# Halving the hand-overs of norms, head outputs and the last product in a diffusion backbone with expert retrieval

## The chip, the cores and the metric

One core of one Trainium2 chip runs the whole kernel. The metric is device time in microseconds, the median of several executions. The profile is one more execution of the same program. Engines are named as in the profile: PE (TensorE, matmuls), PEld (its weight loads), DVE (VectorE), ACT (ScalarE), POOL (GpSimd), SP (SyncE, which here only issues transfers).

## What is computed

Two layers over 256 context tokens and 256 latent tokens of width 1024, all in float32, in tiles of 128 tokens. The reference, cut to its loop:

```python
for l in range(DEPTH):                       # DEPTH = 2
    sh1, sc1, g1, sh2, sc2, g2 = split(silu(c) @ w_ada[l] + b_ada[l], 6)
    h  = rmsnorm(x,  norm_attn_g[l]) * (1 + sc1)  + sh1
    hc = rmsnorm(xc, norm_attn_g[l]) * (1 + sc1c) + sh1c
    y, yc = parallel_mixers(h, hc, ...)      # in projection, MLA (8 heads) and differential (4 heads)
                                             # attention, subnorm of the latter, output projection
    x = x + g1 * y
    h = rmsnorm(x, norm_ffn_g[l]) * (1 + sc2) + sh2
    x = x + g2 * peer_ffn(h, p)              # per token: 8 heads x 16 of 16384 experts, rows u and v
    if not last:                             # the same for the context tokens
        ...
return rmsnorm(x, final_norm_g)
```

`peer_ffn` takes, for each token and each of its 128 picks, a row u (1024) and a row v (1024) of the layer's expert tables: `sum over picks of gelu(u . h) * gate * v`.

## The kernel before

The residual stream X stays on chip as four tiles of 128 tokens x 1024 (0 and 1 the context, 2 and 3 the latent tokens). There are six expert blocks: both pairs in layer 0, the latent pair in layer 1. A block is 128 slots; one slot gathers one expert row pair (8 KB) for each of the 128 tokens, 1 MB, by an indirect transfer of POOL (L681) into a ring of 8 buffers called EXPERT. DVE forms the dot product (L1595), ACT the gelu, the weight and, for three slots of four, a diagonal matrix (L1169, L1171, L1176), PE multiplies that with the v half (L985), and DVE adds the fourth slot itself (L1605). The buffer is then free for the transfer eight slots later.

Everything else is background: norms, projections, attention, the picks of experts. Each engine runs its instructions in one order, written by a planner. `make_plan` lists stages; `front`, `attention` and `outward` give a tile's stages, `weave` mixes slots into them by costs (COST), `keeps_gates` holds a block's close out of the stages between the gates and the use of their rows, and `late` moves slots forward in the orders of DVE and ACT. Three stretches have no slots to mix in: the start until the first picks are there, the pause between the layers (block 3 closed, block 4 without picks), and the end.

The stages that matter here, with their lines:

- `stat` and `norm`. ACT squares X over 1024 columns with a row sum (L1051), takes the root (L1052), DVE inverts it (L1285), ACT scales X into XN (L1063), PE transposes XN in two groups of four 128x128 tiles (L773), and ACT writes them to HT with scale and shift, eight instructions of 128x128 (L1074). PE waits for the whole of XN, and the products that read HT (L844 for the projections, L975 for the expert query) wait for all eight. In `product` that wait is written as a wait for the last bank PE filled, so that it also covers ACT's copies after a `turn` (L1099), which the next product doesn't read.
- `gates`, `hnorm`, `heads`, `out`. DVE puts the gate g1 on diagonals (GD, L1221, called by `diagonals`), PE spreads it to rows by eight matmul records of ones x GD (L860), DVE copies the rows to GROW (L1487). This is done ahead of each half of the output projection (`out` part 0), 512 columns at a time. `hnorm` normalizes the differential heads (L1461, L1126), `heads` transposes the head outputs O, and ACT copies them to HT in two halves (L1135, L1137). After a half of the projection DVE multiplies by GROW and adds to X; only the second half signals `x_ready`.
- `close` adds a block's result to X in two halves, and signals after the second.
- `pick` and `more` are the expert query (two groups of eight products of 128x128), the scores, and the choice of the 16 best.
- `last` is the final norm of a latent tile: square, root, one product over 1024 columns on DVE (L1657), one store of 512 KB (L655).
- `ada`, `adae`, `adat`, `mod` form the modulation vectors from w_ada, 1 MB pieces staged in the EXPERT ring; `adae` is ACT's copy of a product (L1047).

ACT holds one table of functions; where the next function isn't in it, the profile shows ACT_TABLE_LOAD at the line of the instruction that needs it.

## Time and profile before

| | |
|---|---|
| median of 3 runs | 2654.83 us (2645.4 to 2659.23) |
| profiled execution | 2648.58 us, of which span 2645.9 us |
| PE, DVE, ACT, POOL busy | 2068.0, 1854.0, 1149.7, 975.7 us |
| moved by DMA | 980.26 MB, mean 370 GB/s |
| start without slots | 0 to about 238 us |
| pause between the layers | about 1771 to 1915 us |
| last slot's weights to the end | about 2632 to 2646 us |

The busy shares (78% of the span for PE, 70% for DVE) are means over stretches with different limits, and none of them says by itself what sets the time. The page's 40 slices show the DMA engines nine tenths busy or more nearly everywhere but in the three stretches of the table. The chain that ended last puts 21% on transfers, 32% on PE, 25% on DVE and 12% on ACT.

### The profile page before, as it was taken

To read this page: it belongs to the slowest core of one execution; us is meant where nothing else is said; L and a number is where in the kernel's file an instruction comes from. 1 tells how busy PE (TensorE), PEld (TensorE's weight loads), DVE (VectorE), ACT (ScalarE), POOL (GpSimd) and SP (SyncE) were. 2 spreads that over 40 slices of the span, in tenths; PEclk is the share of its full clock that TensorE was granted. 3 is DMA by queue.
4 is the path that set the end of the run, shared out by engine and by line. 5 is a ranking of instruction groups with operands and counts; after the bars stand their busy time and mean duration, and the time that the engine had idled before them with its cause. 6 is when DMAs were issued, how large, how long until landed. Compare 5 with 4: busy or idle time off the path is not lost.

```text
span 2645.9 us, 26377 instructions
## 1 busy us (share of the span) xinstructions
PE 2068.0 (78%) x6888; PEld 1083.2 (41%) x6888; DVE 1854.0 (70%) x4486; ACT 1149.7 (43%) x3047; POOL 975.7 (37%) x916
## 2 busy tenths in 40 slices
PE   5997787876978877888777697879777887677766
PEld 2455443543444445444334244334543444333322
DVE  0146986895557878885979765654597786867776
ACT  2123494344236644753433723432245654433332
POOL 1012333332434333543343444420133443445553
PEclk8998888888989988989889998989888988888988
DMA  8587999997999999999999999996599999999997
GB/s 338 159 298 293 387 385 387 396 395 299 382 389 391 363 409 390 382 383 411 412 409 390 402 415 405 398 405 234 184 412 388 415 351 394 415 382 420 422 421 308
DMA packets 215418, 980.26 MB, mean 370 GB/s; under 512 B 17628, under 2 KB 75512, under 8 KB 116984
## 3 DMA queue, kind: packets, MB, share of 16 engines
q0 software_dynamic: 123648, 855.69, 79.6%
q1 hardware_dynamic: 91640, 123.05, 13.6%
q8 instruction: 55, 0.90, 0.1%
q14 instruction: 75, 0.61, 0.1%
HBM read 977.62 MB, written 1.05 MB: 370 GB/s over the span
## 4 chain that ended last, share of the span: by engine, by line
PE 32%; DVE 25%; DMA 21%; ACT 12%; issue 8%; POOL 1%; SPq 0%; POOLq 0%; DVEq 0%; ACTq 0%
DMA EXPERT<-in_peer_uv,FIX 20%; PE VS L985 12%; PE PA L844 9%; DVE EXPERT L1595 8%; DVE ACC L1605 3%; DVE SCR L1221 2%; PE PA L872 2%; PE PB L773 1%; PE PB L975 1%; ACT L1169 1%; ACT WEI L1171 1%; PE VS L802 1%; PE PB L912 1%; POOL EXPERT L681 1%; ACT DIAG L1176 1%
## 5 line engine op out<-in xcount | busy, mean ns | idle before, releaser
L985 PE MATMUL VS<-EXPERT,DIAG 128*128 128x512 f32 x2304 | 1174.9, 651 | 253.9 <-ACT DIAG L1176 251.7
L681 POOL DMA_INDIRECT EXPERT<-in_peer_uv,FIX x768 | 901.2, 1173 | 1083.5 <-PE VS L985 704.4
L1595 DVE CUSTOM_DVE_ANT_0 EXPERT<-EXPERT,H 128x1024 f32<-128x1024 f32 x768 | 925.0, 1224 | 327.7 <-DMA EXPERT<-in_peer_uv,FIX 318.2
L985 PEld LDWEIGHTS VS<-EXPERT,DIAG 128*128 128x128 f32 x2304 | 458.0, 210 | 829.0 <-issue 480.0
L1169 ACT ACTIVATE GEL<-DOT 128x1 f32<-128x1 f32 x768 | 155.0, 202 | 1028.1 <-DVE DOT L1595 1013.8
L844 PE MATMUL PA<-WT,HT 128*128 128x512 f32 (+2 forms) x720 | 298.6, 560 | 20.3 <-ACT KTD L1099 7.4
L1605 DVE SCALAR_TENSOR_TENSOR ACC<-EXPERT,WEI,ACC 128x1024 f32<-128x1024 f32 x192 | 245.9, 1281 | 25.9 <-ACT WEI L1171 24.0
L1176 ACT ACTIVATE DIAG<-IDN,WEI 128x128 f32<-128x128 f32 x576 | 231.3, 402 | 62.9 <-PE VS L985 44.5
L975 PE MATMUL PB<-HT,WT 128*128 128x128 f32 (+1 forms) x1472 | 212.7, 305 | 39.9 <-issue 36.3
L1171 ACT ACTIVATE WEI<-GEL,GATE 128x1 f32<-128x1 f32 x768 | 226.3, 295 | 24.9
L975 PEld LDWEIGHTS PB<-HT,WT 128*128 128x128 f32 x1472 | 205.4, 216 | 64.8 <-issue 58.7
L844 PEld LDWEIGHTS PA<-WT,HT 128*128 128x128 f32 x720 | 137.2, 194 | 166.0 <-issue 123.4
L673 POOL COPY FIX<-IDX 128x8 uint32 (+1 forms) x96 | 39.7, 413 | 324.6 <-PE VS L985 224.9
L1169 ACT ACT_TABLE_LOAD x115 | 147.5, 1283 | 6.3 <-ACT SCR L1117 0.4
L773 PE MATMUL PB<-IDN,SCR 128*128 128x128 f32 (+1 forms) x382 | 63.8, 319 | 108.0 <-DVE SCR L1376 26.2
L711 POOL DMA_DIRECT2D EXPERT<-in_w_ada x48 | 34.6, 723 | 233.6 <-PE VS L802 159.8
L773 PEld LDWEIGHTS PB<-IDN,SCR 128*128 128x128 f32 (+1 forms) x382 | 51.3, 160 | 141.0 <-ACT SCR L1063 34.8
L956 PE MATMUL PA<-SKT,SCR 128*128 128x128 f32 x192 | 38.9, 337 | 73.4 <-ACT SCR L1154 73.4
L1117 ACT ACTIVATE SCR<-PB,NM 128x512 f32<-128x512 f32 (+1 forms) x96 | 58.7, 614 | 45.1 <-DVE NM L1440 43.2
L956 PEld LDWEIGHTS PA<-SKT,SCR 128*128 128x128 f32 x192 | 31.7, 229 | 102.6 <-ACT SCR L1154 95.6
L1423 DVE TENSOR_REDUCE MX<-PB 128x1 f32<-128x512 f32 (+1 forms) x96 | 55.5, 597 | 21.2 <-PE PB L912 20.6
L1117 ACT ACT_TABLE_LOAD x50 | 64.2, 1283 | 6.4 <-PE PB L912 5.6
(146 smaller groups left out, 1730.0 us busy)
## 6 DMA issues: line engine op xcount, KB each, us to landing
EXPERT<-in_w_ada POOLq DMA_DIRECT2D x48, 1024.0 KB, 11.3
WT<-in_peer_wq SPq DMA_DIRECT2D x92, 512.0 KB
WT<-in_w_in SPq DMA_DIRECT2D x48, 512.0 KB
WT<-in_w_out SPq DMA_DIRECT2D x48, 512.0 KB
EXPERT<-in_peer_uv,FIX POOLq DMA_INDIRECT x768
WT<-in_w_in SPq DMA_DIRECT2D x16, 384.0 KB
WT<-in_w_in SPq DMA_DIRECT2D x16, 288.0 KB
WT<-in_mla_wq_up SPq DMA_DIRECT2D x4, 512.0 KB
```

The costliest lines, as they stand in the source:

```text
L681: pool.indirect_dma_start(out=EXPERT[:, j, :], out_offset=None, in_=a["peer_uv"], in_offset=bass.IndirectOffsetOnAxis(ap=FIX[:, par, j:j + ...
L773: last = nc.tensor.transpose(bank[0:rows, i * P:(i + 1) * P], s, IDN[:, :])
L844: last = nc.tensor.matmul(bank[:, 0:n], ht(k, t), w[:, k % KP, 0:n], start=(k == 0), stop=(k == KD - 1))
L956: last = nc.tensor.matmul(bank[:, c * P:(c + 1) * P], QP[:, r, c, t * P:(t + 1) * P], SKT[:, 2 * l + c, :], start=True, stop=True)
L975: last = nc.tensor.matmul(bank[:, mine], held["w"][k // HP][:, k % HP, c * P:(c + 1) * P], HT[:, k, mine], start=(k == 0), stop=(k == KD - 1))
L985: ins = nc.tensor.matmul(VSUM[n][:, :], DIAG[:, i, :], EXPERT[:, j, D + n * W:D + (n + 1) * W], start=first, stop=last_one)
L1117: ins = nc.scalar.activation(PR[:, h % 2, c, 0:keys], bank[:, 0:keys], ACT.Exp, bias=NM[:, h % 2, c:c + 1], scale=SC_M if h < MH else SC_D ...
L1169: nc.scalar.activation(GEL[:, one], DOT[:, j:j + 1], ACT.Gelu).then_inc(gelu_ready, 1)
L1171: nc.scalar.activation(WEI[:, one], GEL[:, one], ACT.Copy, scale=gate).then_inc(wei_ready, 1)
L1176: nc.scalar.activation(DIAG[:, i, :], IDN[:, :], ACT.Copy, scale=WEI[:, one]).then_inc(diag_ready, 1)
L1595: nc.vector.tensor_tensor_reduce(out=EXPERT[:, j, 0:D], in0=EXPERT[:, j, 0:D], in1=H2[:, b % HB, :], scale=1.0, scalar=0.0, op0=ALU.mult, ...
L1605: nc.vector.scalar_tensor_tensor(out=ACC[:, :], in0=EXPERT[:, j, D:2 * D], scalar=WEI[:, BY_PE:BY_PE + 1], in1=ACC[:, :], op0=ALU.mult, op ...
```

## The change

1. **Norms by halves.** ACT squares 512 columns at a time. The first sum is scaled and gets the epsilon in an added one-column instruction (into NE), and the root takes the second sum with NE as its bias. XN is written and signalled by halves, PE transposes each as it comes, and `x_ready` counts halves, in `out` and in `close`.
2. **HT by halves.** `half_there` waits for four of the eight pieces of a tile's HT (for the first half of the head outputs likewise), before parts 0 and 2 of a product or before k = 0 and 4 of a first expert query. The wait for the last filled bank is gone from `product`, not from `up`.
3. **Gate rows ahead.** Two stages `rows`, one after `hnorm` and one after `heads`, form both halves of the rows and copy them to a GROW of two halves; `out` no longer does. In the two attentions without slots the `gates` stage moves into the attention (`gates_early`). The planner counts a cost of 10 for each `rows`.
4. **Tables asked for ahead.** `table_of` runs a one-column instruction of the function that comes next, with no input to wait for: the root before the norm after the pause's close and before the last one, the exponential before the first attention of either slot-free stretch.
5. **The final product and its store** in two halves each.

The diff, cut:

```diff
 def attention(l, g, t):
     out = [("attn", l, g, t, i) for i in range(-1, MH + DH + 2)]
-    return out + [("gates", l, g, t), ("hnorm", l, g, t), ("heads", l, g, t)]
+    return out + [("gates", l, g, t), ("hnorm", l, g, t), ("rows", l, g, t, 0), ("heads", l, g, t), ("rows", l, g, t, 1)]
+
+
+def gates_early(stages, after):
+    gates = next(s for s in stages if s[0] == "gates")
+    rest = [s for s in stages if s != gates]
+    return rest[:after] + [gates] + rest[after:]
...
-    return s[0] in ("gates", "hnorm", "heads") or (s[0] == "out" and s[3] == 0)
+    return s[0] in ("gates", "hnorm", "heads") or (s[0] == "rows" and s[4] == 0)
...
-    attend, leave, first = attention(0, CTX, 0), outward(0, CTX, (0,)), pick_apart(0, CTX)[0]
-    plan += mingle(attend[:-2], modulation(0, (3, 4, 5))) + [("mod", 0, 2)]
-    plan += attend[-2:-1] + products(1, 0) + [("adae", 1, 0)] + attend[-1:] + [("adat", 1, 0)]
+    attend, leave, first = gates_early(attention(0, CTX, 0), 4), outward(0, CTX, (0,)), pick_apart(0, CTX)[0]
+    plan += mingle(attend[:-4], modulation(0, (3, 4, 5))) + [("mod", 0, 2)]
+    plan += attend[-4:-2] + products(1, 0) + [("adae", 1, 0)] + attend[-2:] + [("adat", 1, 0)]
...
-    keys, attend, leave = front(1, LAT, (1,), queries=False), attention(1, LAT, 0), outward(1, LAT, (0,))
+    keys, attend, leave = front(1, LAT, (1,), queries=False), gates_early(attention(1, LAT, 0), MH + 3), outward(1, LAT, (0,))
...
-    plan += [("adat", 1, 3), sc2[1]] + attend[MH + 4:-1] + sc2[2:] + [("adae", 1, 4), attend[-1], ("adat", 1, 4), ("mod", 1, 2)]
+    plan += [("adat", 1, 3), sc2[1]] + attend[MH + 4:-2] + sc2[2:] + [("adae", 1, 4)] + attend[-2:] + [("adat", 1, 4), ("mod", 1, 2)]
...
                 if stage[0] == "last":
                     t = stage[1]
-                    sp.wait_ge(y_ready, t + 1)
-                    sp.dma_start(out[0, t * P:(t + 1) * P, :], X[:, 2 + t, :]).then_inc(stored, 16)
+                    for half in range(2):
+                        at = slice(half * W, (half + 1) * W)
+                        sp.wait_ge(y_ready, 2 * t + half + 1)
+                        sp.dma_start(out[0, t * P:(t + 1) * P, at], X[:, 2 + t, at]).then_inc(stored, 16)
...
             def norm(stage):
-                pe.wait_ge(xn_ready, tick("norm"))
                 for half in range(2):
+                    pe.wait_ge(xn_ready, tick("norm"))
                     bank = fill_b()
...
+            def half_there(ts, half):
+                for t in ts:
+                    pe.wait_ge(emptied_b, held["ht", t, half])
...
                 if part == 0:
-                    if kind == "out":
-                        gate_rows()
-                    pe.wait_ge(emptied_b, rb.n)
                     held["banks"] = [fill_a() for t in ts]
                     held["fills"] = ra.n
+                if part % (PARTS // 2) == 0:
+                    half_there(ts, part // (PARTS // 2))
...
                 for k in range(KD):
+                    if first and k % (KD // 2) == 0:
+                        half_there(ts, k // (KD // 2))
...
-            def mean_square(tile, place):
-                link(nc.scalar.activation(place, X[:, tile, :], ACT.Square, accum_out=NS[:, :]))
-                nc.scalar.activation(NQ[:, :], NS[:, :], ACT.Sqrt, scale=1.0 / D, bias=EPST[:, :]).then_inc(root_ready, 1)
+            def mean_square(tile, place, changes):
+                for half in range(2):
+                    at = slice(half * W, (half + 1) * W)
+                    if changes:
+                        act.wait_ge(x_ready[tile], 2 * changes - 1 + half)
+                    link(nc.scalar.activation(place[:, at], X[:, tile, at], ACT.Square, accum_out=NS[:, half:half + 1]))
+                    if half == 0:
+                        nc.scalar.activation(NE[:, :], NS[:, 0:1], ACT.Identity, scale=1.0 / D, bias=EPST[:, :])
+                nc.scalar.activation(NQ[:, :], NS[:, 1:2], ACT.Sqrt, scale=1.0 / D, bias=NE[:, :]).then_inc(root_ready, 1)
...
+                if (l, tile, which) == (1, 3, 1):
+                    table_of(ACT.Sqrt)
...
-                nc.scalar.activation(XN[:, t % 2, :], X[:, tile, :], ACT.Copy, scale=NR[:, :]).then_inc(xn_ready, 1)
+                for half in range(2):
+                    at = slice(half * W, (half + 1) * W)
+                    nc.scalar.activation(XN[:, t % 2, at], X[:, tile, at], ACT.Copy, scale=NR[:, :]).then_inc(xn_ready, 1)
...
+            def table_of(function):
+                nc.scalar.activation(IDLE[:, :], EPST[:, :], function)
...
+                if h == 0 and t == 0 and l == g:
+                    table_of(ACT.Exp)
...
-                act.wait_ge(x_ready[2 + t], 4)
+                if t == 1:
+                    table_of(ACT.Sqrt)
                 tick("norm")
-                mean_square(2 + t, XN[:, t, :])
+                mean_square(2 + t, XN[:, t, :], 4)
...
+            def rows(stage):
+                _, l, g, t, n = stage
+                bank = from_a()
+                if n == 0:
+                    diagonals(l, g, 1, 1)
+                nc.vector.tensor_copy(GROW[:, n, :], bank[:, :]).then_inc(emptied_a, 1)
+                dve.wait_ge(emptied_a, ra.n)
...
-                    tt(YT[:, t, :], bank[:, :], GROW, ALU.mult).then_inc(emptied_a, 1)
+                    tt(YT[:, n, :], bank[:, :], GROW[:, n, :], ALU.mult).then_inc(emptied_a, 1)
                     dve.wait_ge(emptied_a, ra.n)
-                    ins = tt(x, x, YT[:, t, :], ALU.add)
-                    if n == 1:
-                        ins.then_inc(x_ready[2 * g + t], 1)
+                    tt(x, x, YT[:, n, :], ALU.add).then_inc(x_ready[2 * g + t], 1)
...
-                x = X[:, 2 + t, :]
-                nc.vector.scalar_tensor_tensor(out=x, in0=x, scalar=NR[:, :], in1=X[:, 0, :], op0=ALU.mult,
-                                               op1=ALU.mult).then_inc(y_ready, 1)
+                for half in HALVES:
+                    x = X[:, 2 + t, half]
+                    nc.vector.scalar_tensor_tensor(out=x, in0=x, scalar=NR[:, :], in1=X[:, 0, half], op0=ALU.mult,
+                                                   op1=ALU.mult).then_inc(y_ready, 1)
```

## Rows read from the trace of the kernel before

**Rows 1.** Busy time by stretch, in 50 us windows: us, each engine, PEclk, DMA share, GB/s.

```profile
250.00:300.00 50.00, 37.19 (x149) 24.41 (x150) 47.82 (x157) 23.01 (x63) 15.82 (x16) 0.81 1.02 411
...
650.00:700.00 50.00, 40.75 (x97) 18.51 (x98) 34.41 (x54) 15.33 (x52) 18.09 (x16) 0.91 0.82 325
...
1850.00:1900.00 50.00, 42.03 (x255) 27.41 (x254) 19.81 (x63) 13.28 (x29) 0.00 (x0) 0.97 0.41 134
...
2550.00:2600.00 50.00, 34.13 (x62) 12.21 (x61) 30.59 (x45) 15.56 (x54) 30.10 (x22) 0.90 1.01 421
```

**Rows 2.** Chain that ended last: start us, us, what; the first 50 us.

```profile
21.04 1.15 ACT SCR L1051 x2
...
41.59 5.35 ACT HT L1074 x15
```

**Rows 3.** Timeline (start us, us, engine line op, operands, [idle before]): copies ahead of products.

```profile
77.38 1.07 ACT L1099 COPY QTD<-PB 128x512 f32<-128x512 f32 x2 [30.45 <-PE PB L773]
...
78.50 14.00 PE L844 MATMUL PA<-WT,HT 128*128 128x512 f32 x32 [0.73 <-ACT QTD L1099]
...
1803.48 4.15 PE L844 MATMUL PA<-WT,HT 128*128 128x288 f32 x16 [0.68 <-ACT KTD L1099]
```

**Rows 4.** Timeline of 204 to 216 us: second norm of the first tile, first expert query.

```profile
203.98 1.06 ACT L1051 ACTIVATE SCR<-X 128x1024 f32<-128x1024 f32 x1 [17.20 <-DVE X L1221]
...
205.69 1.15 ACT L1063 ACTIVATE SCR<-X,NR 128x1024 f32<-128x1024 f32 x1 [0.23 <-DVE NR L1285]
...
207.64 2.90 ACT L1074 ACTIVATE HT<-PB,MOD 128x128 f32<-128x128 f32 x8 [0.33 <-PE PB L773]
...
210.60 5.47 PE L975 MATMUL PB<-HT,WT 128*128 128x128 f32 x32 [1.83 <-ACT HT L1074]
```

**Rows 5.** Groups of instructions with shapes kept apart: busy us, mean ns | idle before.

```profile
L1154 ACT COPY SCR<-PB 128x128 f32<-128x128 f32 x88 | 22.1, 251 | 60.1 <-PE PB L975 60.0
...
L1047 ACT COPY EXPERT<-VS 128x512 f32<-128x512 f32 x12 | 6.9, 578 | 16.1 <-PE VS L802 15.8
...
L1487 DVE COPY SCR<-PA 128x512 f32<-128x512 f32 x12 | 8.2, 684 | 0.0
```

**Rows 6.** Timeline of 1780 to 1795 us, where the stream has paused between the layers.

```profile
1780.66 1.28 ACT L1052 ACT_TABLE_LOAD   x1
...
1781.96 0.29 ACT L1052 ACTIVATE NQ<-NS,EPST 128x1 f32<-128x1 f32 x1
...
1784.51 2.91 ACT L1074 ACTIVATE HT<-PB,MOD 128x128 f32<-128x128 f32 x8 [0.33 <-PE PB L773]
...
1784.78 1.92 PE L802 MATMUL VS<-EXPERT 128*32 128x512 f32 x16
...
1787.47 7.13 PE L844 MATMUL PA<-WT,HT 128*128 128x512 f32 x16 [0.77 <-ACT HT L1074]
```

**Rows 7.** Timeline of 1819 to 1894 us: attention, projection and first expert query.

```profile
1820.47 0.15 DVE L1440 TENSOR_SCALAR NM<-MX 128x1 f32<-128x1 f32 x1
...
1821.08 0.69 ACT L1117 ACTIVATE SCR<-PB,NM 128x512 f32<-128x512 f32 x1
...
1858.91 0.68 DVE L1221 TENSOR_TENSOR GD<-IDN,MOD 128x512 f32<-128x512 f32 x1
...
1862.23 1.09 PE L773 MATMUL PB<-IDN,SCR 128*128 128x128 f32 x8 [1.72 <-DVE SCR L1221]
...
1873.47 1.05 PE L860 MATMUL PA<-GD,ONES 128*128 128x128 f32 x8
...
1889.57 3.84 PE L975 MATMUL PB<-HT,WT 128*128 128x128 f32 x32 [1.83 <-ACT HT L1074]
```

**Rows 8.** Timeline of the last 8 us.

```profile
2639.65 1.28 ACT L1052 ACT_TABLE_LOAD   x1
...
2641.55 1.28 DVE L1657 SCALAR_TENSOR_TENSOR X<-X,NR 128x1024 f32<-128x1024 f32 x1
...
2642.86 0.36 SPq L655 DMA_DIRECT2D out_y<-X  x1
```

56 lines of the change are left out of this document (25 added, 31 removed).

## The prediction

> **What bounds the kernel now.** I read the busy windows first. While slots run, the DMA engines are the limit: in 44 windows of 50 us from 250 to 1750 and from 1900 to 2600 us (the first, the lowest and the last are in [rows 1]) the DMA share is mostly 0.92 to 1.02, and 1.02 is the most any of them shows. In the lowest, 650 to 700 us, it is 0.82. Against 1.02 the 44 windows miss 84.5 us of full transfer (the sum of (1.02 - share) x 50). In the pause between the layers it is another kernel: the share is 0.41 and PE is busy 42.03 of 50 us. So a microsecond taken from a dependent chain in one of the three stretches without slots should move everything behind it, since the stream then starts earlier and has the same bytes to move; a microsecond taken inside the stream counts only in the 84.5 us. Second I read the chain and the timeline of the three stretches, instruction by instruction, for what ended each wait.
>
> **The change part by part.** The sum is made against the profiled execution, 2648.58 us (span 2645.9), which is 6.25 us below the median of 2654.83 that I predict against; I carry the difference over.
>
> *Price of a half on ACT.* A copy of 128 columns takes 0.251 and one of 512 takes 0.578 us [rows 5], so 512 columns fewer save (0.578 - 0.251) / 384 x 512 = 0.44 us. From 1.06 and 1.15 us [rows 4] a half square is about 0.62 and a half XN 0.71. The square's row sum is read out for 0.10 us more on the chain (1.15 for the pair in [rows 2]). A norm then costs ACT 2 x 0.72 instead of 1.15 for squares, 0.30 for the added one-column instruction (as NQ, 0.29 [rows 6]) and 1.42 instead of 1.15 for XN: 0.86 us more. This is the price; what is gained depends on the place.
>
> *Start, to 47 us.* Both first norms lie on the chain in full, from the landing of ctx [rows 2]: 2 x 0.86 = 1.72 us lost. HT of two tiles is 16 pieces of 0.36 us; the product at the end of [rows 2] waits for all and needs, by halves, only twelve: 4 x 0.36 = 1.43 gained. Net 0.29 lost. Then PE waits twice for ACT's copy after a turn, which the next product doesn't read: 0.73 us [rows 3], and the same 0.73 ahead of the product at 94 us: 1.46 gained. The exponential's table before this attention I cost at nothing: PE runs through there with modulation products. The moved gate rows too: PE has no gap in which to put them, the eight records are only at another place.
>
> *Second norm at 204 us.* The first half square hides under the second half of the projection: 1.15 - 0.72 = 0.43 gained. XN by halves brings nothing: HT follows XN's start by 1.95 us [rows 4] with adae's copy in the shadow of PE's transposes; by halves ACT itself is the limit with 1.42 + 0.58 = 2.00 us: 0.05 lost. The query then begins after four pieces of HT instead of eight, and its first 8 records, 8 x 5.47 / 32 = 1.37 us, lie beside the other four [rows 4]. Together 1.75. The start stretch gives -0.29 + 1.46 + 1.75 = 2.9 us.
>
> *Pause between the layers.* Close and norm: the table load of 1.28 us [rows 6] goes under ACT's wait (ACT is idle for microseconds while DVE closes the block), with the same 0.43 and -0.05: HT starts 1.66 earlier. The product started 2.96 after HT's start [rows 6]; now ACT's fourth piece is there after 1.5, but PE still has transposes until about 0.1 after HT's start and then 1.92 us of modulation products [rows 6], so 2.02: 0.94 gained. Sum 2.6. The wait after the turn of kd: 0.68 [rows 3]. The exponential: its operand NM is there at 1820.62 and it runs at 1821.08 behind its table [rows 7]: 0.43 after an issue gap. The GD product of 0.68 us at 1858.91 leaves hnorm's chain [rows 7] (0.60 there) and goes into the attention, where DVE has little slack: I take 0.5 of it, bounds 0 and 0.6. The rows between both halves of the projection, 0.89 of the 1.05 in [rows 7], go; the first rows fall into PE's wait of 1.72 us ahead of `heads` [rows 7]: 0.89 gained. Norm and query as before, at PE's faster level: 0.43 - 0.05 + 8 x 3.84 / 32 = 1.34 [rows 7]. The pause gives 2.6 + 0.68 + 0.43 + 0.5 + 0.89 + 1.34 = 6.4 us.
>
> *End.* The last table load, 1.28 us [rows 8], goes under the wait; the half square gives 0.43. The product of 1.28 becomes two of about 0.70, so the last store is issued 1.28 + 0.43 - 0.12 = 1.6 us earlier and carries 256 KB less, 0.62 us at the 421 GB/s of the last stream window [rows 1]. Store and semaphore took 2645.9 - 2642.86 = 3.04 us [rows 8]. Two issues of 0.36 us don't collide at 0.7 us distance. 2.2 us.
>
> The table load is 1.28 us in the trace and the root follows it at once (1780.66 + 1.28 = 1781.94, root at 1781.96 [rows 6]). The Trainium skill, "ScalarE: Activation LUTs", section "What ACT_TABLE_LOAD costs", adds a drain of 1.38 us to each switch; by that the pause and the end would each give 1.38 more. The trace shows no such gap; so the sum stays without it.
>
> [...]
>
> *Inside the stream.* Twelve of the 18 norms run there: 12 x 0.86 = 10.3 us more of ACT, whose diagonals PE waits for. On the other side are earlier starts of products (four HT pieces, 1.43 us, per norm that PE waits for), the dropped waits behind `turn`, and a wait fewer between the halves of `out`. Each is cheap where DMA is at 1.02 and counts fully only around the windows like 650 to 700 us. I take 0, bounds 10 lost (all of ACT's extra time on the chain) and 10 gained (a good tenth of the 84.5 us). The two `rows` stages shift slots among stages by a place here and there; also in these bounds.
>
> **Sum:** 2.9 + 6.4 + 2.2 = 11.5 us. 2648.58 - 11.5 = 2637.1 for an execution like the profiled one; **2654.83 - 11.5 = 2643.3 us** for the median.
>
> **The rivals.**
> *The stream gains too.* For it: in the window at 650 us DMA starved behind a product and a close, and the chain there goes through HT and PE. Against: ACT pays 0.86 per norm first. With 10 us of the 84.5: 2643.3 - 10 = 2633.
> *The stream pays.* ACT's 10.3 us land on the chain, because slots queue behind `stat` on ACT: 2643.3 + 10.3 = 2653.6, and the whole change looks like nothing. For it: the places where DMA starves are just those where norms run.
> *Slower: DVE is held at the rows.* DVE now waits for PE's rows between hnorm and heads and again after heads, with PE behind slots in its own order and dots queued behind DVE. Place: the four attentions inside the stream, eight waits. Before, DVE was never idle ahead of the copy to GROW (0.0 [rows 5]), so it came there late. To turn the change into a loss over 0.5% the eight waits have to cost 11.5 + 13.3 = 24.8 us, 3.1 us each, more than a slot's share of the stream; at 4 us each the time would be 2643.3 + 32 = 2675.
> *It doesn't do what it says:* the stretches shorten, but landing pieces of w_ada or weights set the pace in the pause. Against: the share of 0.41 there. It would keep the start and the end, 5.1 us: 2649.7.
>
> **How the numbers follow.** Sum as worked out 0.47; the stream gains 0.23; the stream pays 0.15; weights set the pace 0.09; rows hold DVE 0.06. A difference within 0.5%, 13.3 us, is about what a measurement of this kernel can tell from none; the limit is 2641.6, and the forecast lies 1.7 us inside it. Faster: the gaining rival (0.23) and four tenths of the main case (0.18): 0.41. Slower: 0.05. Same: 0.54. The three runs before spread over 14 us, 7 to each side. Range: from 2643.3 down by 10 for the stream and 3 for a PE that stays at its faster level through the query at 210 us (5.47 against 3.84) and the projection, 2630; up to the paying stream and the runs' own spread, 2656.
>
> **What the profile would show.** A root without a table load at the pause's close and at the end; HT's start 1.7 us sooner after the close; no rows between the halves of `out`; the first gather after the start 2.9 us sooner, the first one after the pause a further 6.4 sooner if the stream is as long as before, last dot to end 2.2 us shorter. What remains of the difference is the stream's: if the two stream stretches are longer, the paying rival was right, if DVE idles ahead of the copies to GROW, the slower one. Wrong would be the forecast if ACT's extra 0.86 us per norm came out differently or if the stream didn't pass an earlier start on.

## The result and the profile after

The changed kernel takes **2630.87 us** (median of 7 runs, 2620.14 to 2639.25), the kernel before beside it 2647.33 (7 runs, 2640.21 to 2659.23). The ratio is 0.9933 with an interval of 0.9905 to 0.9961: faster by 0.67%, 17.7 us (10.3 to 25.1). The forecast was 11.5 us and mostly "within 0.5%"; the time lies in the range, 0.9 us above its lower end. Two more comparisons of the same two kernels on other chips gave 0.9939 and 0.9934. The first interval alone would still hold the 11.5 us; the three weighted together give about 17 us (14 to 20, an estimate from the three intervals), which doesn't.

The forecast time was 2643.3, 12.4 us over the measured one. Some 7.5 of that have nothing to do with the change: the kernel before had a median of 2654.83 in three runs and of 2647.33 in seven.

The profiled execution took 2637.23 us, span 2635.3. In the windows of [rows 1], with the same columns:

```profile
250.00:300.00 50.00, 36.74 (x173) 24.50 (x174) 48.53 (x166) 25.02 (x65) 16.62 (x17) 0.90 1.00 390
650.00:700.00 50.00, 50.00 (x130) 23.03 (x129) 28.53 (x46) 13.14 (x46) 20.35 (x20) 1.00 1.02 410
1850.00:1900.00 50.00, 41.23 (x225) 27.68 (x225) 26.00 (x99) 13.16 (x35) 8.52 (x10) 0.93 0.69 245
2550.00:2600.00 50.00, 31.48 (x60) 11.17 (x59) 30.00 (x46) 15.97 (x55) 30.02 (x23) 0.93 1.01 421
```

The picture is the same; the starved place at 650 us has moved (the lowest window of the first stretch is now 600 to 650 us, share 0.66), and 1850 to 1900 already holds the first gathers of block 4. More can be read from the 768 gathers of POOL, which are the same in every kernel here. Their starts cut a trace into five parts: up to the first gather; the first stretch of stream (first to last gather of blocks 0 to 3); from there to the first gather of block 4 (the pause, with some 15 us of tail before the close); the second stretch; and the rest. Three profiles of each kernel (for before, the one shown, one repeated and `pe_busy` below, whose edit puts 0.7 us in ahead of the first query; for after, the one shown and two repeated):

| us | start | first stretch | pause | second stretch | rest |
|---|---|---|---|---|---|
| before | 226.3, 228.9, 228.1 | 1534.3, 1531.9, 1533.7 | 143.6, 147.9, 145.9 | 712.5, 711.2, 707.3 | 29.2, 29.5, 29.5 |
| after | 216.3, 217.5, 219.5 | 1532.2, 1529.0, 1528.0 | 137.1, 137.2, 137.5 | 722.1, 718.4, 718.3 | 27.6, 27.1, 27.4 |
| mean difference | -9.9 | -3.6 | -8.5 | +9.3 | -2.0 |

So the start gives 9.9 us where 2.9 were forecast, the rest what was forecast (2.2), the pause a little more than forecast (6.4; counted from block 3's close to the first gather of block 4 it went from 129.6, 132.0 and 131.3 to 123.5, 121.9 and 123.4, 8.0 less). The two stretches, forecast at zero, are -3.6 and +9.3: not zero, but of opposite signs. The -3.6 is no more than three profiles of one kernel differ by among themselves, the +9.3 is.

Part of the 9.9 is chance. The first product of PE, which waits for the landing of ctx and for the first norms, starts anywhere from 44.2 to 47.0 us in the profiles below, whatever the kernel. From it to the first gather it is 179.3, 184.1 and 182.2 us before and 171.7, 172.2 and 173.5 after: 9.4 us less by the means, 5.8 by the closest pair.

Start (timeline: start us, us, engine line op, operands, [idle before]). The second norm, against [rows 4]:

```profile
197.21 0.63 ACT L1077 ACTIVATE SCR<-X 128x512 f32<-128x512 f32 x1 [5.82 <-DVE X L1260]
...
198.49 1.33 ACT L1094 ACTIVATE SCR<-X,NR 128x512 f32<-128x512 f32 x2 [0.23 <-DVE NR L1324]
199.73 0.56 ACT L1068 COPY EXPERT<-VS 128x512 f32<-128x512 f32 x1
200.19 2.90 ACT L1110 ACTIVATE HT<-PB,MOD 128x128 f32<-128x128 f32 x8
...
201.84 1.13 PE L996 MATMUL PB<-HT,WT 128*128 128x128 f32 x8 [0.44 <-ACT HT L1110]
203.14 2.94 PE L996 MATMUL PB<-HT,WT 128*128 128x128 f32 x24 [0.17 <-ACT HT L1110]
```

The reader is to see the query begin 1.65 us after HT's start instead of 2.96, and its 24 remaining products take 2.94 us, 0.12 each, where 32 took 5.47, 0.17 each: not only earlier, but at the higher of PE's two clock levels. The granted clock is 1.00 from 197 to 212 us, where before it was 0.83 from 210 to 220.

Pause. The first lines answer to [rows 6], the later ones to [rows 7]:

```profile
1767.61 0.29 ACT L1080 ACTIVATE NQ<-NS,NE 128x1 f32<-128x1 f32 x1
...
1769.91 2.90 ACT L1110 ACTIVATE HT<-PB,MOD 128x128 f32<-128x128 f32 x8
...
1772.76 1.06 PE L814 MATMUL VS<-EXPERT 128*32 128x512 f32 x8 [1.40 <-DMA EXPERT<-in_w_ada]
...
1773.75 1.12 PE L861 MATMUL PA<-WT,HT 128*128 128x512 f32 x2
...
1850.44 13.98 PE L861 MATMUL PA<-WT,HT 128*128 128x512 f32 x32
...
1870.54 1.13 PE L996 MATMUL PB<-HT,WT 128*128 128x128 f32 x8 [0.44 <-ACT HT L1110]
1871.85 2.94 PE L996 MATMUL PB<-HT,WT 128*128 128x128 f32 x24 [0.17 <-ACT HT L1110]
```

No table load lies ahead of the root, and HT starts 7.86 us after the close's first add, against 9.91: 2.05 gained, a little over the forecast 1.66. But the product (L861) follows HT's start by 3.84 us: PE waited 1.40 us for a landing piece of `w_ada` and had then 1.06 us of its product to do. It starts 11.70 us after the close's first add in this profile, and 11.69 to 11.72 in every variant of the changed kernel below but `start_late` (13.20), however HT was handed on. Before it was 12.87 in the profile shown, and 14.05 and 14.02 in the other two. The two halves of the output projection are one group of 32 (13.98 us), with no gate rows between.

End, against [rows 8]:

```profile
2630.56 0.29 ACT L1080 ACTIVATE NQ<-NS,NE 128x1 f32<-128x1 f32 x1
...
2631.16 1.42 DVE L1696 SCALAR_TENSOR_TENSOR X<-X,NR 128x512 f32<-128x512 f32 x2
2631.94 1.02 SPq L667 DMA_DIRECT2D out_y<-X  x2
```

### The profile page after: what moved, and what is told of

Same layout as the page of the kernel before. It is cut to its first block, busy times and chain, and to the rows that moved or that the text cites. A ratio compares the mean times of both kernels' runs of the same rounds, so it can differ in the third digit from the quotient of the medians.

```text
span 2635.3 us, 26515 instructions
## 1 busy us (share of the span) xinstructions
PE 2059.6 (78%) x6888; PEld 1073.0 (41%) x6888; DVE 1854.5 (70%) x4488; ACT 1161.4 (44%) x3122; POOL 976.0 (37%) x916
## 3 DMA queue, kind: packets, MB, share of 16 engines
HBM read 977.62 MB, written 1.05 MB: 371 GB/s over the span
## 4 chain that ended last, share of the span: by engine, by line
PE 29%; DVE 24%; DMA 23%; ACT 15%; issue 9%; POOL 1%; SPq 0%; POOLq 0%; DVEq 0%; ACTq 0%
DMA EXPERT<-in_peer_uv,FIX 20%; PE VS L1006 11%; PE PA L861 9%; DVE EXPERT L1634 7%; DVE ACC L1644 3%; ACT L1207 2%; DVE SCR L1260 2%; PE PA L889 2%; ACT L1155 2%; PE PB L996 2%; ACT WEI L1209 2%; ACT SCR L1155 1%; ACT DIAG L1214 1%; PE PB L785 1%; PE VS L814 1%
## 5 line engine op out<-in xcount | busy, mean ns | idle before, releaser
L861 PE MATMUL PA<-WT,HT 128*128 128x512 f32 (+2 forms) x720 | 297.1, 559 | 12.4 <-DMA WT<-in_w_out 4.0
L1209 ACT ACTIVATE WEI<-GEL,GATE 128x1 f32<-128x1 f32 x768 | 226.3, 295 | 24.9
L861 PEld LDWEIGHTS PA<-WT,HT 128*128 128x128 f32 x720 | 137.0, 193 | 159.0 <-issue 132.7
L1634 DVE DVE_READ_ACCUMULATOR2_ANT DOT<- 128x1 f32 x768 | 63.0, 82 | 0.0
```

Of the source, the lines that this page charges most:

```text
L861: last = nc.tensor.matmul(bank[:, 0:n], ht(k, t), w[:, k % KP, 0:n], start=(k == 0), stop=(k == KD - 1))
L1209: nc.scalar.activation(WEI[:, one], GEL[:, one], ACT.Copy, scale=gate).then_inc(wei_ready, 1)
L1634: nc.vector.tensor_tensor_reduce(out=EXPERT[:, j, 0:D], in0=EXPERT[:, j, 0:D], in1=H2[:, b % HB, :], scale=1.0, scalar=0.0, op0=ALU.mult, ...
```

## The experiments

All are timed against the kernel before on their own chip; ratios carry that comparison, profiles are single executions. Three profiles of one kernel scatter by 2 to 5 us in a stretch (the pause after by 0.4), so a smaller distance in a stretch of a single profile shows nothing. The expectations count differently from the table: the first stretch up to block 3's close (14 us more), the pause from there, and the second stretch up to the last add (some 21 us more).

**Both kernels again.**

> The kernel before once more, for its spread and a second profile. Theory A (the 10.0 us that the start stretch lost between the two profiles, from the span's start to the first gather, are mostly PE's clock level and the landing of ctx, which differ from execution to execution): the first gather is issued anywhere from 218 to 228 us, several us away from 226.3, and the ratio is 1.000 within 0.3%. Theory B (the start is the same in every execution, and the change itself brought all 10 us): the first gather is within 1 us of 226.3.

> The changed kernel once more. Theory A (clock and landing by chance): the first gather is issued somewhere from 216 to 224 us, and the difference to the repeat of the kernel before is 3 to 6 us in the start stretch. Theory B (the change brings all of it): within 1 us of 216.3, 10 us ahead of the kernel before. Both: pause between the layers (from the last dot of block 3 to the first gather of block 4) 6 to 7 us shorter than before, end 2 us shorter, ratio 0.993 within 0.003.

> The changed kernel again, unedited, for the other three to be held against: first gather at 216 to 218, pause 122 to 124, end 5.4, first stretch 1544 to 1546 and second 739 to 744 if the two earlier profiles are typical, 2628 to 2632. If single executions scatter by more than that, the second stretch falls outside, as the 733 of the kernel without tables did.

Measured: 1.0007 (0.9992 to 1.0022) for before, 0.9939 (0.992 to 0.9958) and 0.9934 (0.9915 to 0.9952) for after. Their profiles are in the table above. The start is at least 6.8 us shorter in every pairing of them, so the forecast's 2.9 was wrong and not the profile odd.

**The three parts of the change that hand on by halves or leave a wait out, each undone.**

> The changed kernel with the square over 1024 columns again and no NE instruction; XN, HT and all else stay by halves. By the prediction's price (two half squares and NE cost ACT 0.59 us more than one whole square): start 1.2 us shorter than in the changed kernel, second norms, the pause's close and the end each 0.43 us longer, that is 1.3 us longer together with four such places less the start, so 0.5 us longer in the slot-free stretches. Theory that the stream pays for ACT's time: twelve norms x 0.59 = 7 us shorter in the stream, ratio to the changed kernel 0.9975. Theory that the stream doesn't pay: equal within 0.1%.

```diff
-                for half in range(2):
-                    at = slice(half * W, (half + 1) * W)
...
-                    link(nc.scalar.activation(place[:, at], X[:, tile, at], ACT.Square, accum_out=NS[:, half:half + 1]))
...
+                    act.wait_ge(x_ready[tile], 2 * changes)
+                link(nc.scalar.activation(place, X[:, tile, :], ACT.Square, accum_out=NS[:, 0:1]))
```

Measured: 0.9952 (0.9934 to 0.997), beside 0.9939 for the changed kernel on the same chip: no difference that the intervals can tell. Its first stretch is 1523.5 us, shorter than any of five profiles that have the changed kernel's first stretch (1527.1 to 1532.2), its pause 140.1, 3 us longer. That would fit squares in halves that pay outside the stream and cost inside it, with a sum near nothing, but it isn't shown: `rows_late` below, with its squares in halves, has a first stretch of 1525.2.

> The changed kernel with every wait on HT for all eight pieces; the rest stays. By the prediction: start 1.4 us longer ahead of the first product, 1.4 us longer at the first query, pause 0.9 + 0.9 us longer: 4.6 us in sum. Theory that the earlier start of the query also keeps PE at its 2.4 GHz level there: the query at 200 us runs at 5.5 us for 32 records instead of 3.7, 1.7 us more, 6.3 us in sum. Theory that the stream gains from early HT: another 5 us or more on top.

```diff
-                    pe.wait_ge(emptied_b, held["ht", t, half])
+                    pe.wait_ge(emptied_b, held["ht", t, 1])
```

Measured: 0.9968 (0.9954 to 0.9983), 0.3% or 7.7 us slower than the changed kernel beside it (1 to 14 by the two intervals). The start is 221.9 (2.4 to 5.6 back; 174.9 from the first product, 1.4 to 3.2 back), the pause 141.8 (4.5 back), the second stretch 711.1, as before. By this profile HT by halves is worth its forecast 4.7 us and somewhat more outside the stream, and loses part of it inside.

> The changed kernel with the old wait back: a product whose last bank was filled by a turn, not by the norm, waits until ACT has copied that bank. Theory (forecast): 0.73 us each at two places of the start and 0.68 in the pause come back, first gather at 217.8, pause 124; the stream hides its own: 2 us slower than the changed kernel, 2632. Rival (the start is 10 us shorter, not 3, because PE without these gaps is granted 2.4 GHz through it): first gather at 220 or later with PE granted 0.8 instead of 1.0 around 50 to 110 us, 4 us or more slower.

```diff
                 if part == 0:
+                    if rb.n != held["ht", ts[-1], 1]:
+                        pe.wait_ge(emptied_b, rb.n)
                     held["banks"] = [fill_a() for t in ts]
```

Measured: **0.9984 (0.9967 to 1.0002)**. With this one wait put back nearly the whole gain is gone: the ratio lies 0.5% or 13 us (6 to 20 by the intervals) over the changed kernel's. The theory's 2 us falls. The time is the rival's, but not its reason: PE's granted clock is 1.00 from 50 to 110 us here too. Of its twelve executions nine took 2643 to 2651 us and three 2632 to 2634, as fast as the changed kernel; why is open.

**That wait alone.** The kernel before, with nothing changed but the wait:

> The kernel before with one part of the change alone: a product waits for ACT's copies of its own operand HT, not for the last bank that ACT had to empty (which a turn may have filled). Theory (from the changed kernel with that wait put back, which lost 3 to 4 us in the start and 5 in the first stretch): first gather at 222 to 225 us, first stretch 1542 to 1546, pause 0.7 us shorter, 2636 to 2640. Rival (the wait costs only together with the halves, and the kernel that had it back was slow by where its executions fell): first gather at 226 to 228, first stretch 1548, 2644 to 2646.

```diff
-                    pe.wait_ge(emptied_b, rb.n)
+                    for t in ts:
+                        pe.wait_ge(emptied_b, held["ht", t])
...
+                held["ht", stage[3]] = rb.n
```

(the last line is in `heads`, so that the output projection too waits for its own operand).

Measured: **0.9951 (0.9933 to 0.997)**, 13 us (7.9 to 17.7) from a wait that the forecast had at 1.46 + 0.68 us. The first gather is at 222.1, 5.7 us before the mean of before, 4.2 before the profile shown and 6.8 before the repeated one. Outside the stream the two gaps of 0.73 us explain only a part of that. Two views of each kernel, first of the kernel before (repeated), then of `turn_free`: its products, and PE in a 10 us window (us, PE busy, PEclk, DMA share, GB/s).

```profile
76.87 14.00 PE L844 MATMUL PA<-WT,HT 128*128 128x512 f32 x32 [0.73 <-ACT QTD L1099]
92.47 8.01 PE L844 MATMUL PA<-WT,HT 128*128 128x384 f32 x24 [0.73 <-ACT KTD L1099]
113.74 0.70 PE L773 MATMUL PB<-IDN,SCR 128*128 128x128 f32 x4 [2.26 <-DVE SCR L1376]
114.37 4.48 PE L802 MATMUL VS<-EXPERT 128*32 128x512 f32 x24
```

```profile
110.00:120.00 10.00, 7.74 (x41) 0.83 0.37 126
```

```profile
112.87 0.70 PE L773 MATMUL PB<-IDN,SCR 128*128 128x128 f32 x4 [2.26 <-DVE SCR L1378]
113.50 2.78 PE L802 MATMUL VS<-EXPERT 128*32 128x512 f32 x24
```

```profile
110.00:120.00 10.00, 7.74 (x43) 1.00 0.42 147
```

The same 24 products take 4.48 us behind two idle gaps of 0.73 and one of 2.26, and 2.78 us where only the gap of 2.26 is left: 1.7 us of clock (0.83 and 1.00 granted from 110 to 120). All four profiles with the wait in the start (before three times, `turn_wait`) have 4.28 to 4.48. But of the fourteen without it only nine have 2.78; the other five, two of the changed kernel among them, have 3.87 to 4.11. So behind the gaps the products ran slower each time, and without them part of that still comes in some executions.

The rest of the 6.8 us isn't the wait's. From the small products to a score product in the attention it is 16.58 us in the repeated profile and 13.60 in `turn_free` (148.38 to 161.98), which is clock again; but the profile of before that is shown has both gaps and also 13.60:

```profile
152.58 1.06 PE L812 MATMUL PA<-EXPERT 128*128 128x4 f32 x8 [0.41 <-ACT EXPERT L1047]
...
166.18 0.70 PE L912 MATMUL PB<-KTD,QTD 64*128 64x256 f32 x2 [0.56 <-ACT SCR L1117]
```

Counted from the first product, `turn_free` needs 175.4 us to the first gather, 3.9 less than the fastest profile of before, and `turn_wait` 175.4, 1.9 to 3.7 more than the changed kernel's three. So the wait is worth 2 to 4 us in the start.

Inside the stream the same wait is plain to see. PE idles 9.7 us there behind a turn's copy, ahead of products that don't read it (3.21, 0.28, 5.77 and 0.45 us at 691, 718, 1607 and 2045 us; 10.3 in `turn_wait`, nothing in `turn_free` or after), since ACT's copy stands behind the work of slots (three of them at the longest place). That place, in before, and the same eight products in `turn_free`; then PE in 10 us windows of both:

```profile
1605.29 1.54 ACT L1099 COPY KTD<-PB 128x512 f32<-128x512 f32 x3
...
1606.88 4.21 PE L844 MATMUL PA<-WT,HT 128*128 128x288 f32 x8 [5.77 <-ACT KTD L1099]
```

```profile
1596.24 2.10 PE L845 MATMUL PA<-WT,HT 128*128 128x288 f32 x8
```

```profile
1600.00:1610.00 10.00, 4.23 (x10) 0.72 1.02 421
1610.00:1620.00 10.00, 10.00 (x31) 0.93 0.91 341
```

```profile
1600.00:1610.00 10.00, 8.73 (x26) 1.00 1.02 418
1610.00:1620.00 10.00, 6.88 (x22) 1.00 1.02 415
```

The gap is 5.77 us, the eight products behind it take twice as long, and then the transfers fall behind. Against a share of 1.02 the stretch from 1590 to 1650 us misses 1.2 to 1.9 us of transfer in all five profiles that have the wait there, and at most 0.4 in the thirteen others.

> The changed kernel with the dropped wait behind a turn back in the stream alone, not in the start and the pause. Theory (most of the 12 us that this wait was worth lie in the stretches with slots): first gather and pause as in the changed kernel, time 6 us or more over it, 2636 or more, first stretch 1548 or more. Rival (it is the start, where the wait brought 4 to 6 us, and chance for the rest): within 3 us of the changed kernel.

```diff
+                    quiet = (kind, l, g) == ("in", 0, CTX) or (kind, l, g, ts) in (("out", 0, CTX, (0,)), ("out", 1, LAT, (0,)))
+                    quiet = quiet or ((l, g, ts) == (1, LAT, (1,)) and name in ("kd", "vd", "kv"))
+                    if rb.n != held["ht", ts[-1], 1] and not quiet:
+                        pe.wait_ge(emptied_b, rb.n)
```

Measured: 0.9956 (0.9941 to 0.9971) beside 0.9934: 5.8 us slower, 5.0 by the medians, but the intervals leave anything from 0 to 12. Start (217.7) and pause (137.6) are those of the changed kernel, the first stretch 1535.1 us as in `turn_wait` (1535.2) and 3 over the longest of the changed kernel's (though `mixed_late` below reaches 1535.0 without the wait); the second 721.8 (`turn_wait` 722.8) against 718.3 to 722.1. So some 6 us of the wait's 13 lie in the stream by this estimate, where I had counted its drop as hidden. Of them 1.2 to 1.9 are traced, to the place at 1607 us. Start and pause are longer in `turn_wait` by 2 to 4 and 1 to 3 us.

**Is an earlier start passed on?** The second stretch is 9 us longer after, just about what the pause had become shorter. If the stretch took that back, forecasting by stretches would be wrong at its root.

> The changed kernel with the same 84 more products ahead of the first query of the start instead, 10 us. Theory (passed on in full): first gather at 227, first stretch 1544 to 1546, 10 us over the changed kernel, 2640. Rival (the first stretch absorbs part, because it starves less when its tables of work are further ahead): first stretch under 1540, time under 2636.

> The changed kernel with the eight small products of the last modulation vector in the pause, right ahead of the first query there, done 22 times over (84 more at 0.13 us, 10.8 us of PE on the path to the first gather, 0.4 of it in an idle gap); the results are unchanged. Theory (what comes before a stretch is passed on in full): the pause is 10 us longer, the second stretch as long as in the changed kernel, time 10 us over it, 2640. Rival (the second stretch absorbs it, as it seems to have taken back what the change gained in the pause: before 731 us behind a pause of 131, after 741 behind one of 123): second stretch 732 or less, time 2630 to 2634.

```diff
-                for k in range(4):
+                for k in [0, 1, 2, 3] * (22 if (l, n) == (1, 1) else 1):
```

(and with (1, 5) for `pause_late`).

Measured: 1.0087 (1.0071 to 1.0103) and 1.0075 (1.0059 to 1.0092), 2669.17 and 2667.44 us beside 2631.75. The delay came out three times as large as I had worked out, since the line runs for two operands (168 more products, not 84) and each took 0.20 us:

```profile
201.68 35.23 PE L825 MATMUL PA<-EXPERT 128*128 128x4 f32 x176
236.77 6.27 PE L997 MATMUL PB<-HT,WT 128*128 128x128 f32 x32
```

The question is answered all the same. The first gather of `start_late` is 35.5 us later than the mean of after, its stretches are 1527.1 and 718.3 long, and its time is 37.4 us longer. The pause of `pause_late` is 171.1 against 137.3, 33.8 us longer; its second stretch is 716.0, 2.3 under the shortest of after, and its time 35.7 us longer. Neither stretch absorbs more than the scatter. The rival falls, and "what comes before the stream counts in full" stands.

**The longer second stretch.** If not given back, it is made by the change. Seven profiles whose stream hands HT on by halves (after three times, `turn_wait`, `turn_stream`, `start_late`, `pause_late`) have 716.0 to 722.8; the three of before and `turn_free` 707.3 to 712.5; `ht_whole` 711.1. So HT by halves looked like the part that costs there, 7 us, and in after its distance opened between gathers 104 and 120 of block 4, at a norm (57.2 to 57.5 us against 51.7 to 52.6 before; but `pause_late` and `start_late` are as long in all with 51.7 and 47.3 there).

> The changed kernel, but what follows the last norm inside the second stretch (the one of the second latent tile ahead of its joint queries) waits for the whole HT. Theory (the second stretch is 8 us longer in all kernels with halves of HT in it, and the distance opens between its gathers 104 and 120, where this norm lies): second stretch 732 to 736. Rival (it is the sum of several places, the product of the input projection and that of the output too): second stretch 738 to 744. Start, pause and first stretch as in the changed kernel by both.

```diff
+                if stage[1:] == (1, LAT, 1, 2):
+                    held["ht", stage[3], 0] = rb.n
```

Measured: 0.994 (0.9922 to 0.9959), the second stretch 715.6 by gathers (736.7 from first gather to the last add): between both expectations, and gathers 96 to 112 took 57.2 us as in the changed kernel (57.9), not 52.2 as in `ht_whole`. So that norm isn't shown to be the cause; 715.6 is less than 3 us under the shortest of after.

> The changed kernel, with the halves kept only where no slots run: in the twelve norms and four head outputs inside the two stream stretches the square and XN are one instruction each again and the products wait for the whole HT; the first two squares are whole too. Theory (the halves pay in the stream: extra ACT time in stretch 1, the products that start on half of HT in stretch 2): first gather at 216 to 217 us and pause of 122 to 124 us as in the changed kernel, first stretch 1538 to 1542 as with whole squares, second stretch 732 to 735 as with whole HT waits, so 9 to 16 us faster than the changed kernel: 2614 to 2621. Rival (the second stretch is longer by a shift in where slots and stages meet, whatever its norms do, and stretch 1 differs by chance): second stretch 738 to 744, first 1544 to 1546, time within 3 us of 2630.

```diff
+IN_STREAM = [False] * 3 + [True] * 9 + [False] * 2 + [True] * 3 + [False]
+                if IN_STREAM[norms_of("pe")]:
+                    held["ht", stage[3], 0] = rb.n
+                mean_square(tile, XN[:, t % 2, :], changes, IN_STREAM[no] or no < 2)
+                if IN_STREAM[no]:
+                    nc.scalar.activation(XN[:, t % 2, :], X[:, tile, :], ACT.Copy, scale=NR[:, :]).then_inc(xn_ready, 2)
```

Measured: 2624.67 us, 0.9932 (0.991 to 0.9955). Its profile is near what the theory says, stretch by stretch (216.3, 1525.3, 137.5, 714.1; in the count of the expectation 1539.5 and 735.5), and has the shortest span and the lowest median of all. But the time misses the 2614 to 2621 of the theory, and the ratio can't be told from the changed kernel's 0.9934 to 0.9939. If there is a gain over it, it is under 0.5%.

> The changed kernel with the gate rows of both halves made at the head of each half of the output projection again, one from each half. Theory (by the forecast's terms): the rows come back onto the chain in the pause, between the halves and ahead of the first, 0.89 and up to 0.5 us; in the start nothing; the stream as in the changed kernel: 1 to 2 us slower than it, 2631 to 2632. Rival (the moved rows cost the second stretch its 6 to 10 us, since DVE and PE meet at them between hnorm and heads): second stretch back at 733 to 735, time 2622 to 2626.

```diff
-    return out + [("gates", l, g, t), ("hnorm", l, g, t), ("rows", l, g, t, 0), ("heads", l, g, t), ("rows", l, g, t, 1)]
+    out = []
+    for n in range(2):
+        out += [("rows", l, g, ts[0], n)] + [("out", l, g, n, ts, part) for part in range(PARTS)]
```

Measured: 0.9948 (0.9932 to 0.9965). The pause is 0.8 us longer, as its price says; the second stretch is 717.8, so the rows aren't shown to be its cause either.

> The kernel with the halves kept only outside the stream, and in the stream also the gate rows at their old place, at the head of each half of the output projection. Theory (each part pays outside the stream and costs inside it): start, pause and end as in the changed kernel (216.5, 122 to 123.5, 5.3), first stretch 1532 to 1538, second 730 to 735, 2612 to 2620. Rival (the first stretch has no more to give, the 1538 to 1540 seen with whole squares, with mixed halves and with late rows are one and the same level): first stretch 1538 to 1540, 2620 to 2625.

Its edit is that of `rows_late`, for stages in the stream alone, on top of `mixed`. Measured: 0.993 (0.9909 to 0.995), the first stretch 1535.0, 10 us longer than in `mixed` and `rows_late`, which it joins. Neither expectation held for that stretch. The three ratios (0.9932, 0.9948, 0.993) can't be told apart, so whether parts fail to add inside the stream is not shown.

**The tables.**

> The changed kernel without the three instructions that ask for ScalarE's tables ahead. Theory (forecast): 1.28 us back at the end, 1.28 and 0.43 back in the pause: end 6.6, pause 123.6 to 125.2, 3 us slower than the changed kernel. Rival (in the pause the first product waits for a piece of w_ada's product at 11.70 us after the close, whatever HT does): HT starts 1.3 later, the product still at 11.7, pause at most 0.5 longer; 1.7 us slower.

```diff
-                if (l, tile, which) == (1, 3, 1):
-                    table_of(ACT.Sqrt)
-                if h == 0 and t == 0 and l == g:
-                    table_of(ACT.Exp)
-                if t == 1:
-                    table_of(ACT.Sqrt)
```

Measured: 0.9935 (0.9912 to 0.9958), nothing that the time shows. The profile has the load at its place:

```profile
2618.10 1.28 ACT L1080 ACT_TABLE_LOAD   x1
2619.39 0.29 ACT L1080 ACTIVATE NQ<-NS,NE 128x1 f32<-128x1 f32 x1
```

From the last add to the end it is 6.58 us against 5.30 to 5.49 in the changed kernel's three: 1.1 to 1.3. In the pause HT starts 9.56 instead of 7.38 to 8.16 us after the close and the product still at 11.69, the landing of `w_ada`. So the table is worth 1.1 to 1.3 at the end and nothing in the pause. The Trainium skill, "ScalarE: Activation LUTs", section "What ACT_TABLE_LOAD costs", adds a drain of 1.38 us to a switch; the end gained 1.1 to 1.3 and not 2.66, and the root follows the load by 0.01 us, so the trace doesn't agree.

**What sets the clock of the first query.**

> The kernel before, with the four small products of one modulation vector ahead of the first query at about 210 us done three times, so that PE idles less ahead of the query; their results are unchanged. Theory A (the query ran at the lower granted clock, 5.47 us for 32 products, because PE had been idle at its norm): the query takes 3.9 us or less, and the stretch to the first gather keeps its length or loses under 1 us. Theory B (the clock of that place is set by the longer past, the granted 0.8 of the projection before): the query stays at 5.4 us and the stretch is longer by what the eight extra products last. Time within 2 us of the kernel before by both.

```diff
-                for k in range(4):
+                for k in [0, 1, 2, 3] * (3 if (l, n) == (1, 1) else 1):
```

Measured: PE no longer idles, and the query is as slow as before:

```profile
208.19 3.66 PE L813 MATMUL PA<-EXPERT 128*128 128x4 f32 x24
211.71 6.15 PE L976 MATMUL PB<-HT,WT 128*128 128x128 f32 x32
```

At 208 to 212 us the granted clock is 0.72, at 212 to 218 it is 0.62. Theory A falls as it stands: filling the gap with such products doesn't keep the clock up. That idleness has no part in it is not shown, since `start_late` shows that these small products by themselves let the clock fall. Theory B has the right query, but its reason is not borne out either: the projection ahead ran at 1.00. The time, 0.9978 (0.9961 to 0.9994), is 5.8 us under before and within 0.5% of it; its second stretch is the shortest of all, and I have no cause for that.

## Why the prediction was right and wrong

**The step that failed** is the dropped wait behind a turn. It had two terms, 0.73 us twice in the start and 0.68 in the pause, 2.1 in all, and its place in the stream was put under "inside the stream", at zero with the norms. It is worth 13 us (7.9 to 17.7) alone in the old kernel and as much (6 to 20) when put back into the new one. Two things are missing in those terms. First, the stream doesn't hide it. [rows 3] has only the two stretches without slots; in the stream ACT's copy stands behind the work of slots, and PE idled 9.7 us for it, with the clock and then the transfers falling behind at the longest place. `turn_stream` puts this at some 6 us, with 0 not ruled out. Second, I took the idle time before PE for its price in the start. It is 2 to 4 us there, not 1.46, and up to 1.7 us of it is the clock of 24 products 20 us later. My range had 3 us for a clock that stays up, worked out for two other places. In the pause `turn_wait` lost 1 to 3 us against the forecast 0.68. These pieces add up to 9 to 13 us, and only the idle PE and the clock behind it are seen in rows; how the stream's part reaches the time is traced for 1.2 to 1.9 us and open for the rest.

**Range and luck.** That the time fell inside the range is partly luck: the forecast gain was 6 us too small and the base 7.5 us too high, and the lower end was reached by the wait and not by a stream that gains from the halves.

**Start, 2.9 forecast, 9.9 found.** The wait 2 to 4 (1.46 forecast); HT by halves 1.4 to 3.2 from the first product on, where 1.43 + 1.37 were forecast. Of the rest, 1.5 us are a slower clock in the attention of two of the three profiles of before, and 0.6 an earlier first product, both by chance. The norms' price came out as worked out: over the 18 norms, half squares with their sums take 22.2 + 6.7 against 18.8 + 3.4 us, the added instruction 5.3, and XN 1.33 against 1.15 each, together 0.85 us for a norm (0.86 forecast). 1.4 of the 1.7 us for the two first ones are in the chain. The second norm and query: HT to the end of the query went from 8.43 to 5.89 us, 2.5 instead of the 1.37, since its products now run at the upper level (0.12 us each). In `ht_whole` the same query took 6.74 us, in `sq_whole`, which has HT by halves, 5.46, so the halves alone don't secure that level.

**Pause, 6.4 forecast, 8.0 to 8.5 found.** Right in its sum, for partly wrong reasons. The close and norm gave 2.05 (1.66 forecast), of which 1.2 reached the first product in the two profiles shown (2.3 against the other two of before): the piece of `w_ada` came last. This is the rival "weights set the pace", at one place: the low DMA share I held against it is a mean over 50 us, and says nothing of a single landing. The table there is worth nothing for that reason, and neither is HT by halves ahead of the first product (0.94 forecast), which stands at 11.70 us in `ht_whole` too. All that `ht_whole` lost in the pause, 4.5 us, it lost behind that product, where the forecast had 0.96 for the query; 1.2 of it is the query's clock (5.44 against 4.25 us), the rest stays open. The rows (0.89) are gone as forecast, and came back as 0.8 in `rows_late`.

**End, 2.2 forecast, 2.0 found**, the table 1.1 to 1.3 of it.

**Stream, 0 forecast, bounds 10 to each side.** By profiles +5.7 in all, by the medians (20.4 of start, pause and rest against 17.7) +2.7, so within the bounds. It may be two opposite terms: the wait some 6 gained, the norms' extra time and HT by halves lost in exchange. `sq_whole`, `ht_whole` and `mixed` point that way with single profiles only, so it is not shown. What lengthens the second stretch by 9 us stays open: it is not given back from the pause (`pause_late`), not shown to be the rows (`rows_late`) or the last norm (`ht_last`), and mostly absent without HT by halves in the stream (`ht_whole` 711.1, `mixed` 714.1), though `no_tables`, which has them, shows 711.9.

**The slower rival** didn't come: over all twelve copies to GROW DVE idled 4.3 us, in four of them:

```profile
L1525 DVE COPY SCR<-PA 128x512 f32<-128x512 f32 x12 | 8.2, 686 | 4.4 <-PE PA L877 4.3
```

It needed 24.8. **The chances:** with the wait at its real size the sum would have been over 20 us and most of the weight on "faster". The forecast lay 1.7 us on the wrong side of its own limit, and this term's 11 us too few are more than that.

## What to carry to other kernels

A wait that PE doesn't need can cost more than the idle time shown ahead of it, in the granted clock of what follows. Look for it in every stretch, also where transfers set the pace, and price it there from the rows: here the places that I hadn't looked at had 9.7 us of idle PE, those that I had 2.1. And hold a clock that differs against a second profile of the same kernel first: 3.0 us in the attention looked like the wait's price and were scatter. A wait that covers "the last buffer filled" instead of the operand is worth a look in every product. Time taken out ahead of a transfer-bound stream is passed on in full. Inside it single profiles scatter by 2 to 5 us per stretch; only undoing a part with its own timing says what it is worth.

## What the runs showed of the hardware

- PE's clock and small products. In `start_late` PE did nothing but products of 128x4 from 201.68 on, without an idle moment, and the granted clock fell from 1.00 to 0.50 (the level of 1.2 GHz) and stayed there; the query behind ran at that level, 6.27 us, where the changed kernel's took 4.24 (us, PE busy, PEclk, DMA share, GB/s):

```profile
190.00:200.00 10.00, 10.00 (x48) 1.00 0.84 287
200.00:210.00 10.00, 10.00 (x67) 0.72 0.01 2
210.00:220.00 10.00, 10.00 (x49) 0.50 0.00 0
220.00:230.00 10.00, 10.00 (x49) 0.50 0.00 0
```

- 20 us behind two gaps of 0.73 us, 24 products of 128x512 took 4.28 to 4.48 us in all four profiles that have the gaps; without them they took 2.78 in nine profiles and 3.87 to 4.11 in five. The granted clock of the window from 110 to 120 us was 0.83 where they were slow and 1.00 where not.
- Behind an idle gap of 5.77 us eight products of 128x288 took 4.21 us against 2.10 without it (granted clock 0.72 and 1.00 in their windows).
- An instruction of 512 elements on ACT takes 0.62 us for a square and 0.71 for a scaled copy, against 1.05 and 1.15 for 1024.
